# A mixer's queues reordered on three engines, and part of VectorE's work given to GpSimd

## The reference, cut to what matters

```python
def hybrid_mixer(h, w_in, ..., w_out):
    parts = jnp.split(h @ w_in, IN_SPLITS, axis=-1)
    o_nsa = nsa_group(...)    # 8 heads of attention: window, selected and compressed branch, softmax, gates
    o_hg = hgrn2_group(...)   # 4 heads of a gated linear recurrence with decays exp(b[t] - b[s])
    return jnp.concatenate([o_nsa, o_hg], axis=-1) @ w_out
...
b = jnp.cumsum(lf, axis=2)
decay = jnp.exp(jnp.where(tril, b[:, :, :, None, :] - b[:, :, None, :, :], NEG))
a = jnp.einsum('bhtd,bhtsd,bhsd->bhts', qc, decay, kc)
o_intra = jnp.einsum('bhts,bhsv->bhtv', a, vc)
```

## Time and profile before

| | |
|---|---|
| median of 3 runs | 1678.5 us (1677.64 to 1678.93) |
| the profiled execution's own time | 1678.49 us |
| its span in the trace | 1677.2 us |
| TensorE busy | 1640.7 us, 98% of the span |
| VectorE, ScalarE, GpSimd busy | 1189.8, 878.0, 51.2 us |
| the mixer's first scores start, its `w_out` starts | 286.42, 351.75 us from the start |

### The profile page before, as it was taken

The page is one execution under the profiler, slowest core; times in us unless marked ns, Lnnn a source line. Parts: engine busy times, 40 slices in busy tenths (PEclk is TensorE's granted clock), DMA queues, the critical chain, the costliest instruction groups (busy, mean ns, idle before and its releaser), DMA issues.

```text
span 1677.2 us, 24153 instructions
## 1 busy us (share of the span) xinstructions
PE 1640.7 (98%) x9644; PEld 1425.4 (85%) x9644; DVE 1189.8 (71%) x1991; ACT 878.0 (52%) x1521; POOL 51.2 (3%) x87
## 2 busy tenths in 40 slices
PE   8999999999999999999999999999999999999997
PEld 7888899778888888889888888888888998888886
DVE  6766658957666776675877676786667887676777
ACT  5544456755444444455755444655444666454445
POOL 0000000001000000001210000000000000000000
PEclk9999999999999999999999999999999999999999
DMA  9545356034555455545345555545554443565541
GB/s 368 193 186 190 137 188 240 5 135 176 188 188 189 176 204 190 194 160 223 141 171 204 192 193 180 216 184 188 188 189 182 151 145 126 198 222 189 189 163 50
DMA packets 32111, 301.54 MB, mean 180 GB/s; under 512 B 3824, under 2 KB 4352, under 8 KB 6016
## 3 DMA queue, kind: packets, MB, share of 16 engines
q1 hardware_dynamic: 32000, 300.01, 48.6%
HBM read 298.93 MB, written 1.06 MB: 179 GB/s over the span
## 4 chain that ended last, share of the span: by engine, by line
PE 87%; DVE 7%; ACT 3%; issue 1%; POOL 0%; DMA 0%; SPq 0%; DVEq 0%; ACTq 0%
PE bank L477 28%; PE bank L467 27%; PE bank L466 12%; PE bank L456 9%; PE bank L469 2%; DVE w_lo L429 1%; PE bank L507 1%; PE bank L2087 1%; PE bank L580 1%; DVE x L848 1%; PE bank L581 1%; PE bank L605 1%; PE bank L2089 1%; PE bank L584 1%; PE bank L1684 1%
## 5 line engine op out<-in xcount | busy, mean ns | idle before, releaser
L429 DVE TENSOR_TENSOR w_lo<-w_raw,w_hi 128x1024 fp32r<-128x1024 f32 (+4 forms) x539 | 586.9, 1139 | 190.8 <-ACT w_hi L422 190.3
L467 PE MATMUL bank<-xT,w_hi 128*128 128x512 f32 x1920 | 673.8, 396 | 0.3 <-DVE w_lo L429 0.3
L422 ACT ACTIVATE w_hi<-w_raw 128x1024 fp32r<-128x1024 f32 (+5 forms) x543 | 500.3, 981 | 98.0 <-PE bank L477 82.1
L466 PE MATMUL bank<-xT,w_lo 128*128 128x256 f32 x1680 | 468.4, 279 | 0.0
L467 PEld LDWEIGHTS bank<-xT,w_hi 128*128 128x128 f32 x1920 | 351.6, 188 | 69.9 <-DVE w_lo L429 0.5
L466 PEld LDWEIGHTS bank<-xT,w_lo 128*128 128x128 f32 x1680 | 316.7, 189 | 10.4
L795 ACT ACTIVATE ff_silu<-ff_silu 128x256 f32<-128x256 f32 x124 | 51.9, 418 | 387.8 <-DVE ff_silu L948 387.8
L477 PE MATMUL bank<-w_hi,hT_hi 128*128 128x512 f32 x480 | 187.5, 391 | 0.0
L477 PE MATMUL bank<-w_hi,hT_lo 128*128 128x512 f32 x480 | 186.8, 389 | 0.0
L477 PE MATMUL bank<-w_lo,hT_hi 128*128 128x512 f32 x480 | 186.8, 389 | 0.0
L948 DVE TENSOR_REDUCE ff_silu<-bank 128x256 f32<-128x512 f32 x124 | 85.7, 691 | 101.7 <-PE bank L467 100.6
(11 more groups left out here) (398 smaller groups left out, 2170.4 us busy)
## 6 DMA issues: line engine op xcount, KB each, us to landing
w_raw<-in_ffn_a SPq DMA_DIRECT2D x22, 1536.0 KB, 6.6
w_raw<-in_ffn_b SPq DMA_DIRECT2D x22, 1536.0 KB, 6.4
w_raw<-in_ffn_c SPq DMA_DIRECT2D x22, 1536.0 KB, 6.5
w_raw<-in_ffn_d SPq DMA_DIRECT2D x22, 1536.0 KB, 6.6
w_raw<-in_ffn_e SPq DMA_DIRECT2D x22, 1536.0 KB, 6.5
w_raw<-in_ffn_f SPq DMA_DIRECT2D x22, 1536.0 KB, 6.4
gains<-in_gains SPq DMA_DIRECT2D x11, 1024.0 KB, 5.0
w_raw<-in_mla_up SPq DMA_DIRECT2D x8, 1280.0 KB, 5.8
```

Of the source, the lines that this page charges most:

```text
L422: nc.scalar.activation(hi, src, ACTF.Copy).then_inc(w_hi_made, 1)
L429: nc.vector.tensor_tensor(lo, src, hi.bitcast(F32), ALU.subtract).then_inc(w_lo_made, 1)
L466: nc.tensor.matmul(o[:, 0:SEQ], lo[:, c], xT[:, k, 0, :], start=False, stop=False)
L467: ins = nc.tensor.matmul(o, hi[:, c], xT[:, k, :, :], start=(k == 0), stop=(k == KD - 1))
```

## The change

Four edits, all in the mixer:

1. The low part of `w_out1` 0 (two pieces of 1536 columns) is made by GpSimd, behind its `left(1)`, in place of VectorE.
2. GpSimd makes `left` of heads 1, 2 and 3; VectorE keeps `left(0)`.
3. The lead: ScalarE does `decays(0)` and `decays(1)` behind the Gelu, between the copies of the queries, and splits `w_out1` 0 last. VectorE splits `nsa_c` first, then does `away(0)`, `away(1)`, `right(0)`, `left(0)`, `right(1)` ahead of step 0.
4. The steps: ScalarE copies the turned weights of step k - 1 ahead of the exponentials of step k. VectorE does the masks directly behind its `weights`, `away(2)` in parts in steps 1 and 2, `right(2)` and `right(3)` in steps 3 and 5; and gate, mean square and `value_lo` a step earlier.

```diff
-        by_pool = 4 if (name, i) == ("ffn_b", 0) else 0
+        by_pool = {("ffn_b", 0): 4, ("w_out1", 0): 2}.get((name, i), 0)
...
-                pe.wait_ge(left_made, h if h else 1)
-                if h == 1:
-                    pe.wait_ge(left_second_made, 1)
+                pe.wait_ge(left_made, 1)
+                if h:
+                    pe.wait_ge(left_second_made, h)
...
             act_split(first["nsa_c"])
-            decays(0)
             act.wait_ge(mix_tile, 22)
...
                 if j == 3:
-                    act_split(first["w_out1"])
+                    decays(1)
                 if j == 2:
...
+                    decays(0)
...
-            decays(1)
+            act_split(first["w_out1"])
...
             for k in range(STEPS + 2):
                 if k == STEPS:
                     act_split(first["w_out1"] + 1, 0, 1)
-                if k >= 2:
+                if k >= STEPS:
                     value_hi(k - 2)
-                if k == 1:
-                    copy_cross(k)
-                if k < STEPS:
-                    weights(k)
-                if 1 < k < STEPS and k % 2:
+                if k < STEPS and k % 2:
                     copy_cross(k)
                 if k >= 2:
                     output_hi(k - 2)
...
                     keep_output(k - 1)
                     copy_weights(k - 1)
                 if k < STEPS:
+                    weights(k)
+                if 1 <= k < STEPS - 1:
+                    value_hi(k - 1)
+                if k < STEPS:
                     scale_weights(k)
-                if k == 1:
+                if k == 2:
                     decays(2)
...
+            dve_split(first["nsa_c"])
             away(0)
-            dve_split(first["nsa_c"])
+            away(1)
             right(0)
             left(0)
-            away(1)
-            dve_split(first["w_out1"])
+            right(1)
...
             for k in range(STEPS + 2):
-                if k >= 2:
-                    mean_square(k - 2)
                 if k < STEPS:
                     weights(k)
+                    mask_levels(k)
+                elif k == STEPS:
+                    dve_split(first["w_out1"] + 1, 0, 1)
+                    value_lo(k - 2)
+                else:
+                    dve_split(first["w_out1"] + 1, 1)
+                    value_lo(k - 2)
+                if 1 <= k <= STEPS:
+                    mean_square(k - 1)
                 if k >= 2:
-                    gate_output(k - 2)
...
+                    output_lo(k - 2)
+                if k == 0:
+                    scale_gate()
+                elif k == 1:
+                    away_levels(2, range(5))
+                elif k == 2:
+                    away_levels(2, range(5, 7))
+                    away_across(2)
+                    away_levels(3, range(2))
+                elif k == 3:
                     right(2)
...
+                if 1 <= k <= STEPS:
+                    gate_output(k - 1)
                 if k < STEPS:
                     gated_weights(k)
-                if k == 1:
-                    away(2)
+                if 1 <= k < STEPS - 1:
+                    value_lo(k - 1)
...
             left(1)
+            split_lo_pool(first["w_out1"])
             for k in range(STEPS + 2):
                 if k >= 2:
+                    if k in (4, 6):
+                        left(k // 2)
                     pool.wait_ge(ms_made, k - 1)
```

More of the change, by code:

```diff
@@ L1604, in dve_mixer @@
             for k in range(STEPS + 2):
-                if k >= 2:
-                    mean_square(k - 2)
                 if k < STEPS:
                     weights(k)
-                if k >= 2:
-                    gate_output(k - 2)
[L1611 to L1618, removed]
+                    mask_levels(k)
[7 more added lines that the diff above has]
+                    mean_square(k - 1)
+                if k >= 2:
+                    output_lo(k - 2)
[8 more added lines that the diff above has]
+                elif k == 3:
                     right(2)
-                elif k == 3:
-                    left(2)
-                    away_levels(3, range(2))
                 elif k == 4:
```

## The result

The changed kernel takes 1684.75 us (median of 5 runs, 1682.59 to 1685.45); beside it the kernel before took 1678.39 (5 runs, 1677.64 to 1678.93). The ratio on record is 1.0043, with a 95% interval of 1.0032 to 1.0054 (the two medians alone give 1.0038): slower by 0.4%. Its profiled execution took 1684.75 us with a span of 1683.4, so the span is 6.2 us longer.

A forecast was written before the change was run, and what follows sets the result against it. TensorE, busy for 98% of the span, was taken as the bound. Terms +2.5 (lead and steps 0 to 2), +0.2, +3.0 and +2.5 gave +8.2 on 1678.49: 1686.7 us, range 1675.0 to 1690.0.

The forecast's parts named there:

- The multiplies of over 3 us: Sign of being right: VectorE multiplies lasting over 3 us beside GpSimd's two 1536-column subtractions, near 288 to 295 us.
- the idle ahead of the second scores: Sign of being right: TensorE idle 7 to 8 us ahead of scores(1).
- The lead: Ahead of the first scores: VectorE splits nsa_c earlier, TensorE's wait goes, first scores move from 286.42 to 285.45, -0.97 us.
- GpSimd against VectorE: Ahead of step 0: they alternate, then two 3.5 us GpSimd pieces hold VectorE; right(1) ends at 296.0.
- What is late next: Steps 0 to 2: weights(0) starts at 296.0, TensorE stands 7.9 us before scores(1), step 3 starts at 311.7.
- The first part with the lead: Lead and steps 0 to 2 together: +2.5 us, of which 1.8 is lost clock.
- Steps 3 to 7: Mixer steps 3 to 7: two waits of 0.45 us from decays(2) and decays(3); 40.95 against 40.75, +0.2 us.
- Behind step 7: Chain to turn_output(6): step 7's exponentials and VectorE's gates come behind the copies, +3.0 us.
- The clock there: Lower clock after the 3.2 us gap behind step 7: +2.5 us, from bounds of 0 and 3.4.
- Rival (a): GpSimd's long pieces do not hold VectorE ahead of step 0: -0.3 us, 1678.2, chance 0.20.
- Rival (b): Only one long GpSimd piece holds VectorE, five multiplies slip between the two: +5.1 us, 1683.6, chance 0.13.
- (c): No hold by GpSimd's long pieces, and the chain behind step 7 hidden too: -5.8 us, 1672.7, chance 0.15.

The follow-up runs named there:

- x5: The changed kernel with value_hi(6) and value_lo(6) put ahead of the splits of w_out1's second chunk; 1679.53 us, ratio 1.0014.
- x4: The changed kernel with VectorE waiting for each multiply of left(0) and right(1) to end before the next; 1687.78 us in a single run.
- x3: The changed kernel with ScalarE's exponentials of step 7 back ahead of copy_cross(7) and copy_weights(6); 1685.55 us, ratio 1.0052.
- x2: The changed kernel with GpSimd's low part of w_out1 cut into instructions of 256 columns; 1678.52 us, ratio 1.0004.
- x6: The changed kernel with the edits of x2 and x5 together; 1673.5 us, ratio 0.998.
- x7: The changed kernel with scale_gate moved into VectorE's lead, GpSimd's long pieces kept; 1685.81 us, ratio 1.0053.

## Why the prediction was right, and where not

The forecast of 1686.7 was 2 us high; the sum on the span was +8.2 where +6.2 was measured. Part of that closeness is luck: GpSimd's long pieces cost the time, as forecast, but other instructions were held than I had named, and TensorE waited at another place. Of the signs that the prediction named, step 3 (312.31 for 311 to 315), `turn_output(6)` (16.65 us behind the start of step 7 for some 17) and the low clock behind both gaps came. The multiplies of over 3 us and the idle ahead of the second scores did not, and short multiplies were named as a sign of being wrong. By its steps:

- **The lead** (-0.97): -1.59. The wait ahead of `nsa_c` is gone as argued. Another 0.43 us arose ahead of the mixer already, between 198.5 and 208.5 us, where the two traces do the same work: the stretch of low clock there ends sooner in the trace after (at 203 us a matmul of 256 columns takes 0.41 us before and 0.28 after). No edit reaches that stretch, and its clock differs between runs (0.83 in both of these, 1.00 in x5), so this is no gain of the change. The last 0.2 I have not traced.
- **GpSimd against VectorE**: the mechanism, its length (a piece 3.42 us, I had 3.5) and its outcome (two long holds, then idle TensorE and a low clock) were right in kind. The step that failed is "in which VectorE gets 8 done: 5 of `right(1)` are left". I took the one-for-one alternation of the earlier trace rows for a rule, but there GpSimd was under way when VectorE came. Here VectorE was, and GpSimd waited out its whole stream. x4, with the stream broken up, shows the course that I predicted. After step 3, where GpSimd's `left(2)` is first at 319.48, they alternate again: the eight of `right(2)` from 321.31 take 2.75 us instead of 1.7.
- **What is late next**: not `scores(1)`, 7.9 us, but `turn_weights(0)`, 5.68 us. The first part with the lead came to +1.3 for the +2.5 of the text, and two misses offset each other in it: at the full clock step 3 would have started at 312.31 - 4.15 = 308.2 where I had 311.7, and the clock cost 4.15 us where I had taken 1.8.
- **Steps 3 to 7** (+0.2): 0.0. The two waits behind `decays(2)` and `decays(3)` are there, 0.39 us each for the 0.45 of the text. Before, one of 0.35 us stood at 334.71 already, which I had not counted, and step 7 takes 7.78 us after for 8.09 before.
- **Behind step 7** (+3.0): +3.04, through the very chain named. The clock there (+2.5) was a term too large: 1.70 in the profiled run. x3 shows what the text had not seen: undoing the order of step 7 on ScalarE alone gives nothing back, since VectorE's maxima are late too.
- **Rival (a)**, no hold, is excluded by 4.32 and 3.16 us in the profile after and by x2. Its -0.3 is near to what a kernel does that has the same work in short instructions: x2 came to +1.0 us of span. Rival (b), one piece only, is excluded by the second hold, and (c) by the wait of 3.19 us; x6 is about what (c) would have been, 1673.5 for its 1672.7.

The Trainium skill (SBUF: State Buffer, section Who interferes with whom) has the rule on which the forecast leaned, that the one who comes first holds the shared port for a whole instruction. Every pair above with two SBUF inputs bears it out (4.32 us beside 3.42, 3.16 beside 4.39, 3.40 beside 3.48), and so do the biases with one input from PSUM, which kept 0.68 us. The section speaks of one instruction against one, and does not tell who gets the port next. In the runs that is the engine whose stream was running (3.20 and 6.53 us for a single multiply). That the thing they exclude each other from is a port is the Trainium skill's account; the runs show the exclusion alone.

## What to carry to other kernels

Work moved to an idle GpSimd is not free where VectorE reads two SBUF tensors: ask what VectorE does in that very stretch, and cut GpSimd's instructions to the length that its neighbour can wait (256 columns for 1536 took back 5.4 us here). When you put a step earlier in one engine's queue, follow what it displaces to the last wait of the stage: 2.3 us of exponentials behind the copies cost nothing over steps 3 to 7 (40.74 us against 40.75) and 3.0 us behind step 7. Where such a chain has to stay, look for work in it that nobody waits for, as the splits of x5; undoing the reorder on one engine alone moved the gap and did not close it.

## What the runs showed of the hardware

- **Who starves depends on who streams.** A stream of VectorE multiplies at a pitch of 0.2 us kept a GpSimd multiply of 0.45 us waiting for 3.20 us, and with two splits behind it for 6.53 us. The same multiplies, ended one by one, let it in: the eight of `left(1)` took 3.82 us, near the 3.5 of the earlier trace rows. A stream of GpSimd's lets one of VectorE's in after each.
- **A two-column product can last 3.16 us.** Its own length didn't matter here. Those held all read two tensors of SBUF; a reciprocal with one input kept its 0.19 us in the midst of a long piece (x7), and biases with one input from PSUM their 0.68 us beside GpSimd's multiplies.
- **The clock behind a gap.** In x2 gaps of 1.21 and 1.71 us, 8.7 us apart, were followed by a granted clock of 1.00, while the short ones at 197 to 199 us, none over 1.2, went with 0.83 over ten microseconds. Those of 2.65 us and more were followed by 0.50 for a while: some 8 us from the end of the gap of 5.68 us after, and still at 308 to 312 behind gaps of 4.63 (x7) and 5.67 us (x3). The stretch from 195 to 205 us, the same in all kernels, was granted 1.00 in x5 and 0.83 in the nine other traces. With the same gap, `scores(0)` to step 3 took 27.48, 27.52 (x5) and 29.68 us (x3). So a single run's price of a gap is uncertain by 2 us, and I would give the clock a range and not a value.
